# Second layer's modulation rows computed between the grams of the first layer's gated recurrence, passed on through DRAM

## The reference

```python
cond_lat = jax.nn.silu(c)[:, None, :]
cond_ctx = jax.nn.silu(c_ctx)[None, None, :]
for l in range(DEPTH):
    m_lat = jnp.split(cond_lat @ w_mod[l] + b_mod[l], 6, axis=-1)
    m_ctx = jnp.split(cond_ctx @ w_mod[l] + b_mod[l], 6, axis=-1)
    y_lat, y_ctx = _token_mixing(
        _modulate(x_lat, m_lat[0], m_lat[1]), _modulate(x_ctx, m_ctx[0], m_ctx[1]), ...)
    x_lat = x_lat + m_lat[2] * y_lat
    x_lat = x_lat + m_lat[5] * _expert_choice_ffn(
        _modulate(x_lat, m_lat[3], m_lat[4]), moe_router[l], moe_w_gate[l], moe_w_up[l], moe_w_down[l])
    ...   # the same for x_ctx in layer 0
```

## Time and profile before

| | us |
|---|---|
| time before, median of 3 runs | 3751.74 (3747.02 to 3752.83) |
| the profiled execution, its own time | 3750.39 |
| its span from first to last instruction | 3748.3 |
| mean granted TensorE clock | 0.881 of full speed |
| TensorE busy in the span | 3124.3 (83%) |
| VectorE, ScalarE busy | 2258.7 (60%), 1722.3 (46%) |
| L693, both layers: 384 records | 174.5 busy, mean 617 ns |

### The profile page before, as it was taken

How to read it: one execution, slowest core, us unless ns; L and a number is a source line. 1 busy time by engine, 2 the same in 40 slices (tenths; PEclk the granted TensorE clock), 3 DMA queues, 4 the chain that set the end, 5 groups by cost and what they waited for, 6 DMA issues and landing times.

```text
span 3748.3 us, 58124 instructions
## 1 busy us (share of the span) xinstructions
PE 3124.3 (83%) x23555; PEld 2242.7 (60%) x23555; DVE 2258.7 (60%) x2977; ACT 1722.3 (46%) x2276; POOL 397.6 (11%) x100
## 2 busy tenths in 40 slices
PE   7999977866949999999988999777565788888887
PEld 1465767755426666666742566677442566666665
DVE  0150565577356888888851044556764588888887
ACT  1112531223126777777741124312222677777776
POOL 0000000000011211122100000000000222333222
PEclk9999978855979999999999999778568898898988
DMA  9110000000147999999976110000014699999996
GB/s 327 45 53 33 1 1 3 3 2 2 45 195 276 355 360 364 370 353 349 360 279 233 46 56 1 1 3 3 2 46 168 231 361 354 349 342 344 349 351 241
DMA packets 180698, 679.99 MB, mean 181 GB/s; under 512 B 15435, under 2 KB 25759, under 8 KB 180383
## 3 DMA queue, kind: packets, MB, share of 16 engines
q1 hardware_dynamic: 166088, 637.81, 44.5%
q0 software_dynamic: 6144, 20.98, 2.4%
q10 hardware_dynamic: 8283, 18.51, 1.3%
HBM read 656.27 MB, written 20.97 MB: 181 GB/s over the span
## 4 chain that ended last, share of the span: by engine, by line
PE 58%; DVE 16%; ACT 10%; issue 9%; DMA 6%; ACTq 1%; SPq 0%; DVEq 0%; POOL 0%
PE ps L751 12%; PE ps L1923 10%; PE ps L1893 7%; PE ps L1345 5%; ACT hi L2005 4%; PE ps L693 4%; PE ps L1693 4%; DMA gu<-in_moe_w_up 4%; PE ps L1016 2%; ACT arena L2014 2%; DVE gu_lo L2156 2%; PE ps L1931 1%; PE ps L994 1%; PE ps L1007 1%; DVE down_lo L2156 1%
## 5 line engine op out<-in xcount | busy, mean ns | idle before, releaser
L2156 DVE TENSOR_TENSOR gu_lo<-gu,hi 128x2816 fp32r<-128x2816 f32 x256 | 783.4, 3090 | 269.6 <-ACT hi L2005 269.6
L2005 ACT ACTIVATE hi<-gu 128x2816 fp32r<-128x2816 f32 x256 | 643.8, 2550 | 140.2 <-DMA gu<-in_moe_w_up 112.6
L1893 PE MATMUL ps<-hi,xsplit 128*96 128x512 f32 (+3 forms) x2304 | 561.8, 389 | 43.2 <-DVE arena L2170 20.5
L1893 PEld LDWEIGHTS ps<-hi,xsplit 128*96 128x96 f32 (+1 forms) x2304 | 394.9, 176 | 157.8 <-ACT hi L2005 31.0
L751 PE MATMUL ps<-arena 128*128 128x512 f32 (+3 forms) x1440 | 466.9, 484 | 6.9 <-PE ps L751 4.0
L2156 DVE TENSOR_TENSOR down_lo<-down,hi 128x1024 fp32r<-128x1024 f32 (+1 forms) x256 | 403.9, 1618 | 47.1 <-ACT hi L2005 47.1
L1893 PE MATMUL ps<-gu_lo,xsplit 128*96 128x512 f32 (+3 forms) x1536 | 382.0, 384 | 55.3 <-DVE gu_lo L2156 55.1
L2005 ACT ACTIVATE hi<-down 128x1024 fp32r<-128x1024 f32 (+1 forms) x256 | 344.0, 1377 | 159.3 <-PE ps L1923 159.3
L751 PEld LDWEIGHTS ps<-arena 128*128 128x128 f32 x1440 | 270.2, 191 | 196.1 <-issue 172.4
L1893 PEld LDWEIGHTS ps<-gu_lo,xsplit 128*96 128x96 f32 (+1 forms) x1536 | 262.8, 178 | 151.2 <-DVE gu_lo L2156 92.8
L2238 POOL DMA_INDIRECT arena<-xn_rows,row_of x32 | 87.9, 2748 | 2060.9 <-DVE row_of L2147 2056.2
(11 more groups left out here) (291 smaller groups left out, 4270.8 us busy)
## 6 DMA issues: line engine op xcount, KB each, us to landing
gu<-in_moe_w_gate SPq DMA_DIRECT2D x256, 704.0 KB, 9.8
gu<-in_moe_w_up SPq DMA_DIRECT2D x256, 704.0 KB, 6.9
down<-in_moe_w_down SPq DMA_DIRECT2D x64, 2048.0 KB, 13.6
arena<-in_w_mod SPq DMA_DIRECT2D x24, 2048.0 KB, 11.4
down<-in_moe_w_down SPq DMA_DIRECT2D x32, 1536.0 KB, 17.0
arena<-in_w_in SPq DMA_DIRECT2D x6, 2048.0 KB, 7.9
arena<-in_w_out SPq DMA_DIRECT2D x4, 2048.0 KB, 10.4
arena<-in_w_in SPq DMA_DIRECT2D x4, 1536.0 KB, 7.3
```

What stands on the lines that cost most here:

```text
L1893: ins = nc.tensor.matmul(ps[0:lhs.shape[1], 3 * m + b, 0:n], lhsT=lhs, rhs=w[:, c0 + 512 * b:c0 + 512 * b + n], start=(row == 0 and stage ...
L2005: nc.scalar.activation(hi_part(p, is_last), whole(p), ACT.Copy).then_inc(hi_a.sem, 1)
L2156: nc.vector.tensor_tensor(lo_part(p), whole(p), hi_part(p, is_last).bitcast(F32), ALU.subtract) \
```

## The change

Layer 1's rows are no longer made at the start of layer 1. `w_mod[1]` is loaded in layer 0, after the delta rule's last output, in 24 pieces of 256 columns (1 MB each) into a ring of three, `hid_w`. TensorE makes the 24 pieces' 192 products of 256 columns behind the 28 grams of layer 0's recurrence: `AHEAD` puts 6 or 7 of them behind each gram, 96 in each direction. They go to the upper halves of banks 6 and 7. ScalarE copies each finished piece (2x256) to `hid_row` in `mod_rows_out`, called after each of its exponentials, and after every third piece stores 2x768 to `mod_dram`. TensorE's transposes behind the last gram of a direction wait until the direction's last piece is copied.

At the start of layer 1 SyncE loads the 96 rows of 128 from DRAM and the bias as 48 rows of 128, TensorE transposes both (two instructions), and VectorE adds them into `modC`. The two gate rows and their bias are loaded by six small DMAs ahead of the third projection weight, and VectorE adds them before the attention. The first two projection weights of layer 1 no longer wait for the modulation. Layer 0's own modulation is as before.

```diff
+HID = 2 * N_MOD
+HID_STORES = HID // 3
+AHEAD = [(KT * HID // 2) * s // 14 for s in range(15)]
...
+        hid_w = [view(at, KT, 256) for at in (18944, 20992, 40592)]
+        hid_row = [view(at, 768) for at in (17728, 42640)]
...
+                    sp.wait_ge(modout.sem, 16 * HID_STORES)
+                    sp.dma_start(mod_rows, mod_dram.rearrange("v (j p) -> (v j) p", p=P)).then_inc(bmod.sem, 16)
+                    sp.dma_start(bias_rows, t["b_mod"][layer].rearrange("(j p) -> j p", p=P)).then_inc(bmod.sem, 16)
-                for g in range(N_MOD):
+                for g in range(0 if layer else N_MOD):
...
+                    if layer and g == WRING:
+                        sp.wait_ge(scat.sem, scat.n(layer - 1, 16 * NE))
+                        for m, part in enumerate((2, 5)):
...
+                    if g == len(GROUPS) and layer < DEPTH - 1:
+
+                        sp.wait_ge(outv.sem, outv.n(layer, 2 * len(out_tiles(layer))))
+                        for c in range(HID):
+                            if c >= 3:
+                                sp.wait_ge(modmm.sem, modmm.n(1, c - 2))
+                            sp.dma_start(hid_w[c % 3], t["w_mod"][layer + 1][:, c * 256:(c + 1) * 256]
...
+                        act.wait_ge(modmm.sem, modmm.n(1, c + 1))
+                        nc.scalar.activation(hid_row[k % 2][0:2, 256 * third:256 * third + 256], ps[0:2, bank, c0:c0 + 256],
+                                             ACT.Copy).then_inc(modadd.sem, 1)
+                        if third == 2:
+                            act.wait_ge(modadd.sem, modadd.n(1, c + 1))
+                            act.dma_start(mod_dram[:, 768 * k:768 * k + 768], hid_row[k % 2][0:2, :]) \
+                                .then_inc(modout.sem, 16)
...
                 for n in range(1, 12):
                     exps(n)
+                    mod_rows_out(n - 1)
+                for step in range(11, 14):
+                    mod_rows_out(step)
...
+        def pe_next_mod(pe, d, step):
+
+            cT = condT[:, :].rearrange("p (v f) -> p f v", v=2)
+            base = KT * HID // 2 * d
+            for u in range(base + AHEAD[step], base + AHEAD[step + 1]):
+                c, f = divmod(u, KT)
+                bank, c0 = hid_at(c)
+                if f == 0:
+                    pe.wait_ge(mload[c % 3].sem, mload[c % 3].n(1, 16 * (c // 3 + 1)))
+                    if c >= 2:
+                        pe.wait_ge(modadd.sem, modadd.n(1, c - 1))
+                ins = nc.tensor.matmul(ps[0:2, bank, c0:c0 + 256], lhsT=cT[:, f, :], rhs=hid_w[c % 3][:, f, :],
+                                       start=(f == 0), stop=(f == KT - 1))
...
                     ins.then_inc(hgram.sem, 1)
+                    if layer < DEPTH - 1:
+                        pe_next_mod(pe, d, n)
+                if layer < DEPTH - 1:
+                    pe.wait_ge(modadd.sem, modadd.n(1, HID // 2 * (d + 1)))
```

More of the change, by code:

```diff
@@ L329, in trunk_program @@
         modT = sem("modT", 1)
+        modout = sem("modout")
+        gate_in = sem("gate_in")
         modcol = sem("modcol", 1)
@@ L530, in sync_program @@
                     k = layer * LOADS + g
-                    if g < WRING:
+                    if g < WRING and layer == 0:
                         sp.wait_ge(modmm.sem, modmm.n(layer, N_MOD - MRING + g + 1))
@@ L535, in sync_program @@
                         sp.wait_ge(wfree.sem, k - WRING + 1)
+                    if layer and g == WRING:
+                        sp.wait_ge(scat.sem, scat.n(layer - 1, 16 * NE))
+                        for m, part in enumerate((2, 5)):
+                            cols = slice(part * D, (part + 1) * D)
+                            sp.dma_start(gates[:, m, :], mod_dram[:, cols]).then_inc(gate_in.sem, 16)
+                            for r in range(2):
+                                sp.dma_start(gate_bias[r:r + 1, m, :], t["b_mod"][layer:layer + 1, cols]) \
+                                    .then_inc(gate_in.sem, 16)
+                    if g == len(GROUPS) and layer < DEPTH - 1:
[4 more added lines that the diff above has]
+                            sp.dma_start(hid_w[c % 3], t["w_mod"][layer + 1][:, c * 256:(c + 1) * 256]
+                                         .rearrange("(f p) n -> p f n", p=P)).then_inc(mload[c % 3].sem, 16)
                     if g == len(GROUPS):
@@ L685, in pe_mod @@
         def pe_mod(pe, layer):
+            if layer:
+                pe.wait_ge(bmod.sem, bmod.n(layer, 32))
+                nc.tensor.transpose(ps[:, 2, 0:96], mod_rows, ident[0:96, 0:96])
+                nc.tensor.transpose(ps[:, 2, 96:144], bias_rows, ident[0:48, 0:48]).then_inc(modT.sem, 1)
+                pe.wait_ge(modcol.sem, modcol.n(layer, 1))
+                return
             cT = condT[:, :].rearrange("p (v f) -> p f v", v=2)
@@ L792, in dve_mod @@
         def dve_mod(dve, layer):
+            if layer:
+                dve.wait_ge(modT.sem, modT.n(layer, 1))
+                link(nc.vector.tensor_copy(rsum[:, :], ps[:, 2, 96:144]))
+                for m, part in enumerate((0, 1, 3, 4)):
+                    src = ps[:, 2, 0:96].rearrange("p (v j) -> p j v", v=2)[:, KT * part:KT * part + KT, :]
+                    bias = rsum[:, KT * part:KT * part + KT].unsqueeze(2).broadcast_to([P, KT, 2])
+                    ins = nc.vector.scalar_tensor_tensor(modC[:, m, :, :], src, float(m % 2), bias, ALU.add, ALU.add)
+                ins.then_inc(modcol.sem, 1)
+                return
             dve.wait_ge(bmod.sem, bmod.n(layer, 32))
@@ L845, in dve_attention @@
         def dve_attention(dve, layer):
+            if layer:
+                dve.wait_ge(gate_in.sem, 16 * 6)
+                nc.vector.tensor_tensor(gates[:, :, :], gates[:, :, :], gate_bias, ALU.add)
             dve.wait_ge(projev.sem, projev.n(layer, unit_at(layer, 2)))
@@ L1564, in dve_hgrn @@
             dve_gated(dve, layer, 1, 768, hgt[:, :, 256:512])
+            if layer < DEPTH - 1:
+                dve.wait_ge(modout.sem, 16 * HID_STORES)
             nc.vector.memset(ss[:, 60:61], 0.0).then_inc(mixed.sem, 1)
@@ L1579, in act_hgrn, with mod_rows_out @@
                 off = 1 - d
+                def mod_rows_out(step):
+                    if layer == DEPTH - 1:
+                        return
+                    for c in range(HID // 2 * d, HID // 2 * (d + 1)):
+                        if not (step >= 0 and AHEAD[step] < KT * (c - HID // 2 * d + 1) <= AHEAD[step + 1]):
+                            continue
+                        bank, c0 = hid_at(c)
+                        k, third = divmod(c, 3)
+                        if third == 0 and k >= 2:
+                            act.wait_ge(modout.sem, 16 * k)
+                        act.wait_ge(modmm.sem, modmm.n(1, c + 1))
[5 more added lines that the diff above has]
+                                .then_inc(modout.sem, 16)
                 def exps(n):
```

9 lines of the change are left out of this document (added).

## The result

The changed kernel takes 3725.22 us (median of 5 runs, 3714.30 to 3726.09), against 3751.74 for the kernel before on the same chip. The ratio is 0.9926 (95% interval 0.9914 to 0.9937): 0.7% faster, 4 us from the forecast of 3721 and inside the range. The profiled execution took 3725.82 us.

The account below looks back on a forecast made before the run. Layer 1's start was taken as bound by the modulation's products, layer 0's recurrence mostly by VectorE. From 3750.4 us, minus 74.0 plus 44.4 gave 3721, with bounds 3708 to 3738 and a range of 3702 to 3750.

Parts of the forecast that it names:

- The clock in the mixture: Layer 0's recurrence: grams mixed with products run at full clock, where grams alone had stayed at 0.50.
- Rival (a): Layer 0's recurrence: the clock stays at 1.2 GHz in the mixture, 3821 us; chance 0.07 in part, 0.03 in full.
- A direction: Layer 0's recurrence, each direction: 62.3 us net against 40.1, so 22.2 us more, 44.4 for both.
- Handover: Layer 0's recurrence: the transposes wait for ScalarE's copy of the last piece, 0.6 us a direction.
- Cold start: Layer 0's recurrence: the first gram and products run at half clock, losing 4.0 us a direction, bounds 2 and 6.
- The shorter tail: Layer 0's recurrence: the transposes and the products behind them run warm for a while, 1.0 us less a direction.
- The start of layer 1: Layer 1's start: the modulation leaves the chain, the tokens' path remains, and projections start 74.0 us sooner.
- rival (c): Layer 1's start: smaller gain; tokens' load still 17.4 us, 3726, or another wait, 3746; chance of the dear end 0.05.
- The transposes' clock: Layer 1's start: transposes alone raise the clock after idleness, so projections lose nothing; by the skill's rule some 2 us.
- The sum: Whole kernel: 3750.4 us profiled, less 74.0 at layer 1, plus 44.4 in layer 0, gives 3720.8, so 3721.
- (b): Layer 0's recurrence: ScalarE's order of copies and exponentials sets the pace; each further 0.5 us a step adds 14 us, 3735; chance 0.04.
- (d): Layer 0's recurrence: grams and products overlap better, 1.0 us a gram and 2 us of cold start, 3711; within the forecast's 0.81.

Follow-up runs that it names:

- the products' placement: The changed kernel with 65 of the 192 products moved into TensorE's idle stretches, ahead of the first grams and behind the states: 3695.76 us, ratio 0.9856.
- both edits: The changed kernel with 65 products in idle stretches and the tokens' load at layer 1's start cut into six: 3689.22 us, ratio 0.9842.
- the pause filled: The kernel with 65 products in idle stretches and six token loads, plus four products moved behind gram 2 of each direction: 3683.97 us, ratio 0.9819.

## Why the prediction was right, step by step

**The clock in the mixture**, the choice that decided between 3721 and 3821: full clock, as taken; it came up at about 809, 4.6 us after the first gram. Rival (a) is out for this mixture, and the run with all products in one piece shows what it would have been built on: the grams alone hold 0.50. But the reason was weaker than it read. "Products raise the clock" does not hold at any share: with an eighth of them it stayed down, with a quarter it went both ways.

**A direction**, 63.3 us to the transposes: measured 64.7 and 64.3. Its terms: grams 14 x 1.37 = 19.2 us where 16.8 stood, at the upper side of the bounds of 1.0 and 1.44; what keeps a gram from half of its 2.0 us was not shown. Products 96 x 0.446 = 42.8 for 41.9. Handover 0.5 for 0.6. Cold start about 2.2 (what is left of 64.7) for 4.0, at the lower bound, because the second gram was already fast. The grams' miss of 2.4 us and the cold start's of 1.8 nearly cancel; that is luck. The shorter tail gave 1.7 and 1.1 us for 1.0. Net 22.8 and 23.0 us for 22.2.

**The start of layer 1**, 74.0 us: measured 75.8. From the load's issue to the projections 33.5 us for 35.4: the load 11.2 for 11.9, squares 6.3, roots 3.1 with handovers, multiplications 4.1, transposes to projections 8.7 for 10.0. The time beside it had been read rightly as the tokens' path; the 17.4 us of the earlier trace rows, rival (c)'s cheap end, became 11.2 with the w_mod loads gone from beside it. Its dear end, rows from DRAM in the way, is out by some 28 us. The gates' six DMAs took 2.2 us of SyncE's queue for 3, and VectorE's addition took 2.3 us, under its wait.

**The transposes' clock.** The row of the kernel before was followed and it held: after 32.7 us without work, transposes alone brought it up. Windows of the changed kernel:

```profile
2024.50:2026.50 2.00, 1.79 (x9) 1.82 (x10) 0.06 (x1) 0.24 (x1) 0.00 (x0) 0.50 0.00 0
2026.50:2029.00 2.50, 2.50 (x18) 2.31 (x17) 1.27 (x2) 1.63 (x3) 0.00 (x0) 0.76 0.00 0
2029.00:2033.00 4.00, 3.01 (x24) 2.49 (x24) 3.47 (x6) 3.06 (x6) 0.00 (x0) 1.00 0.00 0
```

The rule of the Trainium skill weighed there (TensorE: Matmul & The Clock Gate, "Part 4: PE-mode transpose") would have the projections begin at half clock; their first 64 products take 27.72 us, to the hundredth what they took in the earlier trace rows. The trace disagrees with the rule.

**The sum.** 3750.4 - 75.8 + 45.8 = 3720.4 by the measured stretches, 0.4 us from the sum on record; this nearness too is luck, since 1.8 us too little gain at layer 1 stands against 1.4 us too little cost in layer 0. The profiled execution has 3725.8. The step that failed is the last one, that the rest stays as it is: 5.7 us came in unchanged code. Whether the change has a part in them is open. From layer 1's projections to the end, in the order of this document, the nine experiments' traces have 1687.6, 1684.1, 1691.9, 1690.7, 1685.0, 1691.8, 1687.4, 1688.2 and 1692.1 us, where before had 1688.8 and after 1690.6: there the kernel before lies among the others. In layer 0, from the output projection's first product to the experts' last, it does not: its one trace has 976.4 us, the changed kernel's 980.6, and the nine experiments' 978.3 to 982.7. So a cost of some 2 to 6 us there that all ten share is not excluded. What moves the experts by such amounts was not settled.

The bounds on record do not follow from their own terms. With grams of 1.0, a cold start of 2 and a load of 10.5 the sum is 3720.8 - 5.6 - 4.0 - 1.4 = 3709.8, not 3708; with 1.44, 6, 17.4 and half of (b) it is 3720.8 + 6.7 + 4.0 + 5.5 + 7 = 3744, not 3738. The measured time lies inside either. The reading that TensorE has 14 x 0.35 us to spare at 1.2 GHz leaves out its two longer waits; in the run with all products in one piece, whose grams take as long, it was busy for 32.4 of their 40 us. The sum does not use it.

Rival (b) is out by the run with deferred copies; (d), 3711, fell with the 1.37 us of a gram.

## What to carry to other kernels

Work that is to fill a stage bound by another engine should be put between that stage's own instructions, in slots sized by the waits there and ahead of its first instruction: the same 192 products made the two directions 86 us longer behind the grams and 49 spread evenly, and the kernel's time fell by a further 26 us or so (by the ratios 0.9926 and 0.9856) where 65 of them stood in TensorE's idle stretches at the stage's ends. Filler has a second effect on TensorE: it can bring the granted clock up for the small products around it, and where filler was taken out it fell again behind pauses, so read the clock of the stretch before costing either. And when a stall is removed, price the next chain link by link; here it was another load's path, and cutting that load saved the next 4.6 us.

## What was not expected of the hardware

**Less work took longer.** The reason is the level of the clock. One eighth of the products: 47.1 us a direction at 0.50. One half: 45.0 at 1.00. One quarter: 41.9 and 44.1, with changes of level inside. In the kernel before, with none, 40.1 at 0.50.

**A small gram gains less than the clock.** It depends on what stands beside it. Back to back, 64x64 records take 41.7 ns each at 0.50 (four grams, 8.01 us) and 30.1 at 1.00 (the stage of L1345), a ratio of 0.72. Between products, from the gram's start to the next product's, a gram takes 2.40 us at 0.50 (one eighth of the products) and 1.37 at 1.00, a ratio of 0.57. Neither is one half. The 256-column products go from 0.94 to 1.0 us down to 0.446, a ratio near one half.

**A pause and a fall.** Each fall of the clock inside a direction that the experiments' timelines show stands behind a pause of TensorE: 2.10 and 1.66 us with the products' placement, 1.65 and 2.50 with both edits, 2.11 with the pause filled, 3.00 with a quarter of the products. With 2.50 and 3.00 the next gram was slow at once; behind the others it took its 1.44 to 1.49 us and the products after it were slow. So the dip of 0.60 at 889 to 893 in the last run follows the pause of 2.11 us that ends at 887.15. But a pause does not always bring a fall: behind 1.65 us in the first direction with the placement alone, and behind 2.12 us in the second with both edits, the records kept their full pace. The stage of L1345 holds 1.00 while it is busy for 8.86 of 10 us, with its idle time in gaps too. What tells the pauses with a fall from those without stays open.
